# Layer 1's dilated attention: the products with V one tile behind, with two places for each turned map

## The reference, cut to what matters

```python
D_BRANCHES = ((128, 1), (512, 4), (2048, 16))
s = jnp.einsum('bcnqhd,bcnkhd->bcnhqk', qb, kb) * (dh ** -0.5)
s = s - slopes[:, None, None] * (delta * dil)
s = jnp.where(valid[:, None], s, -jnp.inf)
e = jnp.exp(s - m); den = jnp.sum(e, axis=-1, keepdims=True)
o = jnp.einsum('bcnhqk,bcnkhd->bcnqhd', (e / den), vb)
# the branches' outputs are then weighted by their shares of the summed denominators
```

## Time and profile before

| | us |
|---|---|
| median of 3 runs | 2261.44 (2258.38 to 2263.11) |
| the profiled execution's own time | 2265.03 |
| its span | 2263.1 |
| mean granted TensorE clock | 0.988 of full |
| layer 1's attention, first turn to the turns of Y | 148.3 |

### The profile page before, as it was taken

One profiled execution on the slowest core, in us unless ns is written; L12 is line 12 of the kernel. 1 busy time (PEld: TensorE's weight loads), 2 busy tenths in 40 slices (PEclk: granted clock), 3 DMA queues, 4 the chain that ended last, 5 costly groups with the idle time before them and its releaser, 6 DMA issues.

```text
span 2263.1 us, 29909 instructions
## 1 busy us (share of the span) xinstructions
PE 2193.0 (97%) x10632; PEld 1834.4 (81%) x10632; DVE 1259.3 (56%) x1765; ACT 878.8 (39%) x1433; POOL 792.2 (35%) x533
## 2 busy tenths in 40 slices
PE   8999897999999999999999998989999999999999
PEld 7886787888888887888888887888888888887887
DVE  4245775775555554558313246655775555654555
ACT  4124873443333333435311136651443333334433
POOL 1022542266677772002000032200366676662000
PEclk9999999999999999999999998999999999999999
DMA  5021120045554447674111111102055555547665
GB/s 180 10 79 29 38 85 19 19 132 192 193 194 163 163 163 269 195 240 151 38 38 56 38 65 38 38 9 67 20 165 192 192 194 167 167 149 275 191 194 195
DMA packets 218906, 282.92 MB, mean 125 GB/s; under 512 B 11440, under 2 KB 120496, under 8 KB 218800
## 3 DMA queue, kind: packets, MB, share of 16 engines
q1 hardware_dynamic: 218512, 281.45, 38.3%
q10 hardware_dynamic: 288, 0.05, 0.0%
HBM read 199.67 MB, written 73.40 MB: 121 GB/s over the span
## 4 chain that ended last, share of the span: by engine, by line
PE 73%; issue 19%; DVE 4%; ACT 2%; POOL 2%; DMA 1%; SPq 0%; POOLq 0%; DVEq 0%; ACTq 0%
PE PS L1301 12%; PE PS L1302 12%; PE PS L1303 12%; PE PS L1328 6%; PE PS L1329 6%; PE PS L1330 6%; PE PS L1014 4%; PE PS L924 3%; PE PS L926 3%; PE PS L925 3%; PE PS L998 2%; PE PS L978 1%; POOL QRS L838 1%; PE PS L979 1%; PE PS L942 1%
## 5 line engine op out<-in xcount | busy, mean ns | idle before, releaser
L1822 DVE TENSOR_TENSOR LINEl<-LINE,HIGH 128x1024 fp32r<-128x1024 f32 x154 | 193.7, 1264 | 169.7 <-ACT HIGH L1359 169.4
L1359 ACT ACTIVATE HIGH<-LINE 128x1024 fp32r<-128x1024 f32 x154 | 162.5, 1059 | 236.0 <-PE PS L1330 226.8
L1328 PE MATMUL PS<-HIGH 128*128 128x512 f32 x616 | 241.5, 392 | 7.0 <-DVE LINEl L1822 7.0
L1330 PE MATMUL PS<-HIGH,LINEl 128*128 128x512 f32 x616 | 240.6, 391 | 0.0
L1329 PE MATMUL PS<-LINEl,HIGH 128*128 128x512 f32 x616 | 240.6, 391 | 0.0
L1822 DVE TENSOR_TENSOR SLOTl<-BLOCKS,RING 128x512 fp32r<-128x512 f32 x168 | 155.7, 927 | 98.9 <-ACT RING L1359 94.2
L807 POOL TENSOR_TENSOR ST<-ST 128x512 f32<-128x512 f32 x132 | 195.5, 1481 | 31.5 <-DMA ST<-in_ffn_w_down 22.8
L1359 ACT ACTIVATE RING<-BLOCKS 128x512 fp32r<-128x512 f32 x168 | 105.9, 630 | 227.7 <-PE PS L1303 225.7
L1822 DVE TENSOR_TENSOR SLOTl<-SLOT,RING 128x512 fp32r<-128x512 f32 x126 | 136.1, 1080 | 86.8 <-ACT RING L1359 86.5
L838 POOL TENSOR_TENSOR QRS<-QMS,EXPO 128x8 f32<-128x8 f32 x32 | 52.0, 1639 | 375.4 <-DVE QMS L1990 375.2
L1328 PEld LDWEIGHTS PS<-HIGH 128*128 128x128 f32 x616 | 116.3, 189 | 32.3 <-DVE LINEl L1822 8.3
(11 more groups left out here) (304 smaller groups left out, 5678.3 us busy)
## 6 DMA issues: line engine op xcount, KB each, us to landing
LINE<-hidden SPq DMA_DIRECT2D x154, 256.0 KB, 2.7
hidden<-HID SPq DMA_DIRECT2D x44, 512.0 KB, 4.5
ST<-in_ffn_w_down SPq DMA_DIRECT2D x44, 512.0 KB, 4.0
sums<-ST SPq DMA_DIRECT2D x22, 1024.0 KB, 6.2
hidden<-ST SPq DMA_DIRECT2D x22, 1024.0 KB, 6.8
LINE<-sums SPq DMA_DIRECT2D x88, 256.0 KB, 3.0
BLOCKS<-in_ffn_w_gate SPq DMA_DIRECT2D x42, 512.0 KB, 4.0
BLOCKS<-in_ffn_w_up SPq DMA_DIRECT2D x42, 512.0 KB, 5.2
```

The lines of the kernel that those rows point to most:

```text
L1328: pe.matmul(dst, hi[:, 0, ts], hi[:, 1, :], start=j == 0 and not adds_on, stop=False, skip_group_check=adds_on)
L1330: pe.matmul(dst, lo[:, 0, ts], hi[:, 1, :], start=False, stop=j == NJ - 1, skip_group_check=adds_on).then_inc(dn_pe, 1)
L1359: return nc.scalar.activation(dst, src, ACT.Copy, **kw)
L1822: return v.tensor_tensor(dst, src, hi.bitcast(F32), ALU.subtract)
```

## The change

Both products with V stand one tile behind. TensorE's list for tile n becomes: turn 0 for n, score 0 for n+2, weigh 0 for n-1, turn 1 for n, score 1 for n+2, weigh 1 for n-1, and after the last tile both products of tile 31. Each map's PT has a second place (PTB0 and PTB1), used by odd tiles; they lie where QK held the first unit's queries and keys, and the copies wait until those are stacked. The turns now wait across the units' borders for the three banks. On ScalarE the order of the list stays, with a wait for the product of two tiles before. On VectorE the reciprocals and the scaled outputs come a tile later: scaled 0 for n-1 stands after turned 0 for n and ahead of biased 1 for n+1, scaled 1 for n-2 after biased 0 for n+1, and the reciprocals come ahead of these.

```diff
         PR = [[at(f"PR{m}{b}", [P, TOK], F32, oHL + 16 * KB + 8 * KB * m + 4 * KB * b) for b in range(2)] for m in range(2)]
+
+        PTL = [[PT[m], at(f"PTB{m}", [P, TOK], F32, oC + 16 * KB * m)] for m in range(2)]
         YJ = at("YJ", [P, P], F32, oK + 4 * KB)
...
                 for c in range(i // 4 + 1):
-                    if L == 1 and TURNS.index((m, i, c)) >= 3:
-                        m0, i0, c0 = TURNS[TURNS.index((m, i, c)) - 3]
+                    if L == 1 and (u > 0 or TURNS.index((m, i, c)) >= 3):
+
+                        u0, k0 = divmod(len(TURNS) * u + TURNS.index((m, i, c)) - 3, len(TURNS))
+                        m0, i0, c0 = TURNS[k0]
                         if c0 == 0:
-                            pe.wait_ge(t_ea[m0][1], g + i0 + 1)
+                            pe.wait_ge(t_ea[m0][1], NT * u0 + i0 + 1)
                         else:
-                            pe.wait_ge(t_ed[m0][1], h + i0 - 3)
+                            pe.wait_ge(t_ed[m0][1], 4 * u0 + i0 - 3)
...
-            def weigh(L, m, u, g, h, i):
-
-                pe.wait_ge(t_ea[m][L], g + i + 1)
+            def weigh(L, m, n):
+
+                u, i = n // NT, n % NT
+                pe.wait_ge(t_ea[m][L], n + 1)
                 if L == 1 and i >= 4:
-                    pe.wait_ge(t_ed[m][1], h + i - 3)
-
+                    pe.wait_ge(t_ed[m][1], 4 * u + i - 3)
                 if L == 0:
-                    pe.wait_ge(o_ok[0][0], g + i + 2)
+                    pe.wait_ge(o_ok[0][0], n + 2)
                 else:
-                    pe.wait_ge(o_ok[1 - m][1], g + i + 2 + m)
+                    pe.wait_ge(o_ok[1 - m][1], n + 2 + m)
                 w, off = (P, u * P) if L == 0 else (HD, u * P + HD * m)
+                turned = PTL[m][i % 2] if L else PT[i % 2]
                 for j in range(i + 1):
-                    last = pe.matmul(weighed(L, m, i), PT[m if L else i % 2][:, P * j:P * j + P], V[:, j, bass.ds(off, w)],
+                    last = pe.matmul(weighed(L, m, i), turned[:, P * j:P * j + P], V[:, j, off:off + w],
                                      start=(j == 0), stop=(j == i))
                 last.then_inc(o_pe[m][L], 1)
...
-                            turn(1, 0, g, h, i)
+                            turn(1, 0, u, i)
                             if i == NT - 2 and more:
                                 pe.wait_ge(staged[1 - b], 128 + 64 * (u // 2 + b + 1))
                                 pe.wait_ge(stack_lo, following + 3)
                             if more:
                                 score(1, 0, b, g, i + 2)
-                            turn(1, 1, g, h, i)
-                            weigh(1, 0, u, g, h, i)
+
+                            if g + i > 0:
+                                weigh(1, 0, g + i - 1)
+                            turn(1, 1, u, i)
                             if i == NT - 2 and more:
                                 pe.wait_ge(stack_lo, following + 4)
                             if more:
                                 score(1, 1, b, g, i + 2)
-                            weigh(1, 1, u, g, h, i)
+                            if g + i > 0:
+                                weigh(1, 1, g + i - 1)
+                    for m in range(2):
+                        weigh(1, m, TILES0 - 1)
...
                         w = min(HALF, P * (i + 1))
-                        src, to = turn_bank(1, m, i, 0)[:, 0:w], PT[m]
+                        if g + i >= 2:
+                            act.wait_ge(o_pe[m][1], g + i - 1)
+                        elif i == 1:
+                            act.wait_ge(stack_lo, STACK_AT[1] + len(STACK0))
+                        src, to = turn_bank(1, m, i, 0)[:, 0:w], PTL[m][i % 2]
...
-                        def turned(m, i):
-                            if i >= 4:
-                                dve.wait_ge(t_pe[m][L], g + i + 3)
-                                w = P * (i + 1)
-                                v.tensor_copy(PT[m][:, HALF:w], turn_bank(1, m, i, 1)[:, 0:w - HALF]).then_inc(t_ed[m][1], 1)
-                        def scaled(m, i):
-                            c = m + 2 * (i % 2)
-                            dve.wait_ge(s_ex[m][1], g + i + 1)
-                            att.link(v.reciprocal(RDN[:, c:c + 1], DEN[:, c:c + 1]))
-                            dve.wait_ge(o_pe[m][1], g + i + 1)
-                            v.tensor_scalar(Y[:, i, bass.ds(u * P + HD * m, HD)], weighed(1, m, i), RDN[:, c:c + 1], None,
-                                            ALU.mult).then_inc(o_ok[m][1], 1)
+                    def turned(m, n):
+                        u, i = n // NT, n % NT
+                        if i >= 4:
+                            dve.wait_ge(t_pe[m][1], n + 3)
+                            dve.wait_ge(o_pe[m][1], n - 1)
+                            dve.wait_ge(stack_lo, STACK_AT[1] + len(STACK0))
+                            w = P * (i + 1)
+                            v.tensor_copy(PTL[m][i % 2][:, HALF:w], turn_bank(1, m, i, 1)[:, 0:w - HALF]).then_inc(t_ed[m][1], 1)
+                    def denominator(m, n):
+                        c = m + 2 * (n % 2)
+                        dve.wait_ge(s_ex[m][1], n + 1)
+                        att.did(v.reciprocal(RDN[:, c:c + 1], DEN[:, c:c + 1]))
+                    def scaled(m, n):
+                        u, i = n // NT, n % NT
+                        c, off = m + 2 * (n % 2), u * P + HD * m
+                        att.wait()
+                        dve.wait_ge(o_pe[m][1], n + 1)
+                        v.tensor_scalar(Y[:, i, off:off + HD], weighed(1, m, i), RDN[:, c:c + 1], None, ALU.mult).then_inc(o_ok[m][1], 1)
+                    for n in range(TILES0):
+                        u, i = n // NT, n % NT
+                        b, g, more = u % 2, NT * u, n + 1 < TILES0
                         def next_bias(m):
                             dve.wait_ge(s_mx[m][1], g + 9)
                             bias(m, 1 - b, 2 * u + 2 + m)
-                        for i in range(NT):
-                            if i == NT - 1:
-                                att.wait()
-                            more = u + 1 < UNITS or i + 1 < NT
-                            if more:
-                                biased(0, b, g, i + 1)
-                            if i == NT - 2 and u + 1 < UNITS:
-                                next_bias(0)
-                            if i > 0:
-                                scaled(1, i - 1)
-                            turned(0, i)
-                            if more:
-                                biased(1, b, g, i + 1)
-                            turned(1, i)
-                            scaled(0, i)
-                            if i == NT - 2 and u + 1 < UNITS:
-                                next_bias(1)
-                            if i == NT - 1:
-                                scaled(1, i)
+                        if n > 0:
+                            denominator(0, n - 1)
+                        if i == NT - 1:
+                            att.wait()
+                        if more:
+                            biased(0, b, g, i + 1)
+                        if i == NT - 2 and u + 1 < UNITS:
+                            next_bias(0)
+                        if n > 1:
+                            scaled(1, n - 2)
+                        turned(0, n)
+                        if n > 0:
+                            scaled(0, n - 1)
+                            denominator(1, n - 1)
+                        if more:
+                            biased(1, b, g, i + 1)
+                        turned(1, n)
+                        if i == NT - 2 and u + 1 < UNITS:
+                            next_bias(1)
+                    denominator(0, TILES0 - 1)
+                    scaled(1, TILES0 - 2)
+                    scaled(0, TILES0 - 1)
+                    denominator(1, TILES0 - 1)
+                    scaled(1, TILES0 - 1)
```

More of the change, by code:

```diff
@@ L1143, in _ @@
                                 score(0, 0, b, g, i + 2)
-                            if i > 0:
-                                weigh(0, 0, u, g, 0, i - 1)
-                            elif u > 0:
-                                weigh(0, 0, u - 1, g - NT, 0, NT - 1)
+                            if g + i > 0:
+                                weigh(0, 0, g + i - 1)
                             if more:
                                 score(0, 1, b, g, i + 2)
-                            turn(0, 0, g, 0, i)
+                            turn(0, 0, u, i)
                             if g + i >= FILL_FROM:
                                 out_block(g + i - FILL_FROM)
-                    weigh(0, 0, UNITS - 1, NT * (UNITS - 1), 0, NT - 1)
+                    weigh(0, 0, TILES0 - 1)
                 else:
                     for u in range(UNITS):
-                        b, g, h = u % 2, NT * u, 4 * u
+                        b, g = u % 2, NT * u
```

(16 more changed lines are left out.)

11 lines of the change are left out of this document (5 added, 6 removed).

## The result

The changed kernel takes **2282.61 us**, the median of four runs (2279.39 to 2283.96); beside it the kernel before took 2261.92, also four runs. The ratio is 1.0092, 95% interval 1.0075 to 1.0110: slower by 20.7 us. The forecast was +15.7 and 2277.1, with a range from 2267 to 2288. The profiled execution took 2283.64 us, its span 2281.8, which is 18.7 more than the span of before. The steps are judged against that 18.7, as they were worked out from one execution too. By the medians the rise is 20.7: the two profiled executions lie 3.1 (before) and 1.0 (after) above their medians.

What follows compares the result with a forecast made beforehand. TensorE, busy 97% of the span, was taken to bound the kernel. New gaps +28.9, old idle time -10.7 and tail -2.5 gave +15.7 us, a median of 2277.1 us from 2261.44, range 2267 to 2288.

Steps and rivals of the forecast that it cites:

- unit 0: 6.7 come, 2.1 go: Unit 0: new gaps at tiles 1 to 6 and a small one add 6.7 us; old idle time of 2.1 leaves.
- unit 1: 7.8 come, 3.4 go: Units 1 and 2, each: new TensorE gaps add 7.8 us, old idle time of 3.4 us leaves.
- unit 3, tiles 0 to 5: 6.6 come, 1.8 go: Unit 3 before its last tiles: new gaps add 6.6 us, idle time of 1.8 us leaves.
- tail: From turn 0 of tile 30 on: 2.5 us gained, between about 1 and 4.1 depending on the clock.
- TensorE's own work, 32.2 us a unit: TensorE's product matmuls, turns and scores in a unit: 16.0 + 8.0 + 8.2 = 32.2 us.
- The ring: Biased 1 (n+1) waits behind scaled 0 (n-1) on VectorE, and TensorE's score 1 for biased 1: +28.9 us in 26 large gaps.
- reciprocal to biased: VectorE's step from the reciprocal to biased, in no trace row: taken as 0.15 us, between 0 and 0.24.
- L1019's waits for PT: Sign to look for in the profile after: TensorE's waits for PT at this line, L1014 before, must be gone.
- Idle time of before goes: All TensorE idle time of before in the stage's units was taken to leave: 10.7 us.
- Tile 6: ScalarE's and GpSimd's chain runs beside the new gap, ending within about 0.1 us: nothing added, 1.15 us idle.
- the rival that it falls often: TensorE's clock: eight to ten more falls at 1.24 us give +10 to +12, about 2288 us; chance 0.12.
- The rival of a gain: Scaled 0 ahead of biased 1 on VectorE doesn't bind and waits vanish: -10.5 us, 2250.9 us; chance 0.06.

Runs made afterwards that it cites:

- e1: The changed kernel with scaled 0 of n-1 moved behind biased 1 of n+1 on VectorE, the lag and PT places kept; 2255.72 us, ratio 0.9965.
- e6: The changed kernel with two more 128x1 reciprocals, into an unused place, between the reciprocal of map 1 and biased 1; 2283.82 us, ratio 1.0098.
- e2: The changed kernel with the next unit's table for map 0 made behind scaled 1 instead of ahead of it, at tile 6; 2279.62 us, ratio 1.0095.
- after_again: The changed kernel once more, without an edit; 2283.89 us, ratio 1.0094, its profiled execution with a span of 2278.6 us.
- e10: The changed kernel with a 128x512 copy from f32 to bf16, into scratch, between the reciprocal and biased 1; 2312.34 us, ratio 1.0215.
- e4: The kernel before, without lag or new places, with its scaled 0 put ahead of biased 1 on VectorE; 2339.74 us, ratio 1.0344.
- e3: The changed kernel with scaled 0 behind biased 1 and, at tile 6, the table for map 0 behind scaled 1; 2254.17 us, ratio 0.9961.

## Why the prediction was right, and where its terms were off

The ledger of the profiled execution, by its span:

| step of the prediction | forecast | measured |
|---|---|---|
| start of the stage | 0 | +0.2 |
| unit 0: 6.7 come, 2.1 go | +4.6 | +6.7 |
| unit 1: 7.8 come, 3.4 go | +4.4 | +4.0 |
| unit 2: the same | +4.4 | +5.3 |
| unit 3, tiles 0 to 5: 6.6 come, 1.8 go | +4.8 | +4.7 |
| tail | -2.5 | -2.2 |
| sum | +15.7 | +18.7 |

The measured column takes each window less its work (32.2 or the new order's, above), after less before: unit 0 (39.87 - 28.65) - (36.71 - 32.2) = 6.7; unit 3 (28.96 - 22.4) - (23.32 - 21.5) = 4.7; the tail (16.27 - 12.65) - (15.84 - 10.0) = -2.2.

**TensorE's own work, 32.2 us a unit,** stands: no kernel went below it, and the best came to 33.75.

**The ring: right, in mechanism, place and size.** Forecast 28.9 us in 26 gaps; e1 shows 27 for the order of two instructions. In the profile after, what the prediction named is there: 24.2 us for NMX in 25 pieces of at most 1.1 us, the output followed within 0.2 us by reciprocal and biased, and units of 40.9 (39 to 41 were forecast). The link that was in no row, reciprocal to biased, was taken as 0.15, between 0 and 0.24. It measured 0.07, so the gaps of tiles 3 to 5 and 7 came out 0.07 to 0.08 smaller than forecast, 1.1 us in all; those of tiles 0 and 2 came out 0.1 larger. e6 shows that the tiles follow this chain one for one. One of the signs that were named did not come: L1019's waits for PT should have gone, and the weight loads still have 3.1 us of them in 6 pieces (2.6 in 6 before). The three longest are tile 6's, which e2 takes away by an edit on VectorE (1.1 in 3 are left).

**Idle time of before goes: nearly right.** The sum let all 10.7 us go. In e1, without the ring, a unit still has 2.2 us idle, of which 1.25 are at tile 6 (5.70 for 4.45) and 0.56 at tile 0. With the ring in place most of it seems to pass beside the gaps, since the units came out near the forecast; that is argued, not shown.

**Tile 6: the step that was off.** The prediction set ScalarE's and GpSimd's chain beside the ring and added nothing. Measured are 2.07 us idle instead of 1.15. The cause is on VectorE: its list has the table of 1.28 us ahead of scaled 1, with the lag the product of map 0 waits for that output, and the table took 1.78 beside GpSimd. The rows of the table and of the output's place in the list were there to be read; the prediction counted what stands between weigh 0 and biased, but not what stands between weigh 1 and scaled 1. That GpSimd would lengthen the table was in no row of before, where all took 1.27 to 1.29. By e2 it is 0.75 us a unit, 2.3 in three.

**The clock: right for units 1 and 2, short for unit 0.** Against the rival that it falls often (2288), units 1 and 2 were granted 1.00, though TensorE was idle for 8.7 of 40.9 us. The Trainium skill's rule, taken into the prediction from "TensorE: Matmul & The Clock Gate", Part 1, would have made the sum larger by the number of falls; here the trace goes the other way: no fall came in those units, and one that was there before, in unit 1, is gone, worth 1.2. Unit 0 had its half-rate stretch from the stage's start until 1382.1 instead of 1376.1, which is the extra 2.1 us of its row. after_again has it until 1375.3, and there unit 0 is (37.63 - 28.65) - 4.5 = +4.5, as forecast. So the extra belongs to the execution. But the +4.5 is in part luck, as tile 6's 0.9 is in it too. And the margin was thin: e10 puts 0.33 us more into each gap and loses some 16 us to the clock, e4 more, and two of e2's six executions were 10 and 15 us slower than its others at a lower clock, with the changed kernel's gaps.

**The tail** came to -2.2, near the middle of -4.1 to -1, its clock 0.89. In after_again it is (14.95 - 12.65) - (15.84 - 10.0) = -3.5 at a clock of 1.00, so the middle was hit by the execution.

**The rival of a gain** was a ring that doesn't bind: 2250.9. e1 takes the ring away by an edit and comes to 2255.7, or 7.1 below before where 10.5 was worked out. Most of the missing 3.4 is idle time that the rival had left out: 0.56 at tile 0 and 1.25 instead of 0.9 at tile 6, in three units 2.7. e3 gets 8.6.

**The error in sum**, 3.0 us, is by the ledger unit 0's +2.1 (the clock), unit 2's +0.9, unit 1's -0.4 (the same +0.9 less the fall of 1.2 that before had there), and +0.4 for start, unit 3 and tail. Unit 2's +0.9 is tile 6's +0.92, 0.75 of it by e2; its other tiles, from -0.08 to +0.13, sum to nothing. Had the profile been that of after_again, the rise would be 2278.6 - 2263.1 = 15.5, and the forecast 0.2 off. That nearness would be luck: tile 6's 2.8 in three units would be made up by the fall that before had in unit 1, a tail at the full clock and a shorter half-rate stretch in unit 0.

## What to carry to other kernels

A lag takes a wait off the engine that produces and puts it on the queue that consumes: before an output is moved a tile back, write down, for each engine that works in order, what is queued behind it and who waits for that. An instruction that will have to wait belongs behind those that others wait for, even where that engine is idle for more than a third of the time; here one line's place is worth 27 us, and the whole lag 8. Hold tile times against tile times, since an effect of 0.9 us a unit can be plain there and hidden in the total by a clock stretch of 2 us.

## What the runs showed of the hardware

**VectorE and GpSimd hold each other.** The table (a `scalar_tensor_tensor` of 128x1024 with DIST and MASK in SBUF) takes 1.28 us alone. It took 1.78 when GpSimd's 64x256 part of 0.72 began 0.02 us before it (after) and 1.55 when the part began 0.26 before (e3). In e1 the table began first, at 1460.21, and kept its 1.28, while the part at 1460.55 took 1.53. So in these three the one that began second was the one that was held. e10's cast, 0.41 alone, took up to 1.66. Biased and the outputs, which read PSUM, and the 128x1 reciprocals kept their time beside GpSimd in after. The Trainium skill, page "SBUF — State Buffer", section "Who interferes with whom", says that a VectorE instruction with two inputs in SBUF contends with a GpSimd one that reads SBUF, and calls the port pair that they share an exclusive lock. The trace agrees that there is a hold and with whom, but it is shorter than the overlap: 0.50 of 0.70 us in after, 0.27 of 0.47 in e3, 0.81 of 0.94 in e1.

**Many gaps of 1 us can leave the clock alone, and somewhat longer ones don't.** Gaps of about 1.0 us in every tile of 2.8 to 6.5 us (and 2.1 in two pieces at tile 6) left the granted clock at 1.00 (2.4 GHz) in units 1 and 2 of both profiled executions. With 0.33 us more in each, and longer ones at tiles with GpSimd's work, it was 0.83 to 0.86; with waits of up to 1.7 us and no lag 0.75. There the fall costs more than the gaps that bring it, some 16 of 28 us in e10. The length of the gaps alone doesn't decide: before was at half clock from 1410.3 to 1413.7, behind the border into unit 1, where after with more idle time had the full clock.

**Small VectorE instructions overlap.** The 128x1 reciprocal lasts 0.15 us, but the next instruction starts 0.07 after it (in e6 the two more took 0.06 each in unit 2, though more in tile 3 of unit 1). A chain is to be priced by such a pitch, not by the duration.

**The named releaser can be the wrong one.** The 0.56 us wait was put down to ScalarE's copy, and went away when two instructions changed places on VectorE. Where an instruction waits for several semaphores, look at every one of them in the timeline.
